# A diffusion-backbone layer on one core: the front of the kernel in a new order, and the first head's modulation chunk moved from VectorE to TensorE

## What is computed

```
m = jax.nn.silu(cvec) @ w_mod + b_mod              # 2048 -> 6 x 2048, for c and for c_ctx
sh_a, sc_a, g_a, sh_f, sc_f, g_f = jnp.split(m[..., None, :], 6, axis=-1)
h = _rmsnorm(s, p['norm_pre_mix']) * (1.0 + sc_a) + sh_a
proj = h @ p['w_in']
qkv = jax.nn.silu(_dwconv(proj[..., COL_K:COL_BETA], p['conv_qkv']))
beta, g = _gdn_gates(proj[..., COL_BETA:COL_Z], p['a_log'], p['dt_bias'])
h = jnp.sin(f1 * (z @ w1 + b1))                    # three such layers, then @ w4, times a window
filt = h * jnp.tile(window, (1, 2))
out = jnp.concatenate([o, y], axis=-1) @ p['w_out']
s = s + g_a * _rmsnorm(out, p['norm_post_mix'])    # then the feed-forward sub-layer
```

## Time and profile before

| | us |
|---|---|
| median of 3 runs | 1856.74 (1856.66 to 1858.7) |
| profiled execution, its own time | 1847.59 |
| its span | 1845.9 |
| PE busy | 1695.5 |
| DVE busy | 1190.6 |
| ACT busy | 727.8 |

### The profile page before, as it was taken

The page is one execution under the profiler, slowest core; times in us unless marked ns, Lnnn a source line. Parts: engine busy times, 40 slices in busy tenths (PEclk is TensorE's granted clock), DMA queues, the critical chain, the costliest instruction groups (busy, mean ns, idle before and its releaser), DMA issues.

```text
span 1845.9 us, 30924 instructions
## 1 busy us (share of the span) xinstructions
PE 1695.5 (92%) x11344; PEld 1512.1 (82%) x11344; DVE 1190.6 (65%) x1778; ACT 727.8 (39%) x1199; POOL 124.2 (7%) x231
## 2 busy tenths in 40 slices
PE   4879699998999899999998599999999998999995
PEld 1237598998989798999998388888888888999994
DVE  2545687786878687777787755555555555565464
ACT  2153334434344434443333344444444443333332
POOL 2000201100111101000000000000000001010010
PEclk9979899998999999999999699999999999999998
DMA  9884342523333242532597044445554446676671
GB/s 356 303 328 157 139 155 80 183 99 138 122 131 137 105 154 84 197 115 92 220 346 298 1 181 183 182 182 189 199 197 187 182 182 207 230 267 208 228 238 57
DMA packets 61424, 334.04 MB, mean 181 GB/s; under 512 B 8395, under 2 KB 12550, under 8 KB 33489
## 3 DMA queue, kind: packets, MB, share of 16 engines
q1 hardware_dynamic: 41808, 257.97, 38.2%
q0 software_dynamic: 18656, 70.35, 10.7%
q10 hardware_dynamic: 864, 4.47, 0.7%
HBM read 328.56 MB, written 4.19 MB: 180 GB/s over the span
## 4 chain that ended last, share of the span: by engine, by line
PE 85%; DVE 6%; DMA 4%; ACT 2%; DVEq 1%; issue 1%; ACTq 0%; SPq 0%
PE o L455 13%; PE o L456 13%; PE o L457 13%; PE o L462 9%; PE g L462 9%; PE o L463 4%; PE g L463 4%; PE g L531 2%; PE g L526 2%; PE g L534 2%; DMA xc<-in_xc_t 2%; PE g L795 1%; ACT w_hi L431 1%; DMA w_raw<-in_w_gates_t 1%; DMA w_raw<-in_w_down_t 1%
## 5 line engine op out<-in xcount | busy, mean ns | idle before, releaser
L436 DVE TENSOR_TENSOR w_lo<-w_raw,w_hi 128x2048 fp32r<-128x2048 f32 (+1 forms) x225 | 472.7, 2101 | 244.6 <-ACT w_hi L431 238.0
L431 ACT CAST w_hi<-w_raw 128x2048 fp32r<-128x2048 f32 (+1 forms) x225 | 394.7, 1754 | 362.3 <-PE o L457 331.5
L455 PE MATMUL o<-h_hi,w_hi 128*128 128x256 f32 (+1 forms) x896 | 305.6, 341 | 0.0
L457 PE MATMUL o<-h_hi,w_lo 128*128 128x256 f32 (+1 forms) x896 | 288.1, 322 | 0.0
L456 PE MATMUL o<-h_lo,w_hi 128*128 128x256 f32 (+1 forms) x896 | 287.8, 321 | 0.0
L462 PE MATMUL o<-h_hi_lo,w_hi 128*128 128x512 f32 x704 | 247.2, 396 | 12.6 <-DVE h_hi_lo L1782 12.6
L462 PE MATMUL g<-h_hi_lo,w_hi 128*128 128x512 f32 x704 | 245.1, 394 | 0.0
L455 PE MATMUL o<-ff_hi,w_hi 128*128 128x256 f32 x704 | 202.9, 288 | 11.0 <-ACT w_hi L431 5.7
L457 PE MATMUL o<-ff_hi,w_lo 128*128 128x256 f32 x704 | 202.0, 287 | 0.0
L463 PE MATMUL o<-h_hi_lo,w_lo 128*128 128x256 f32 x704 | 195.9, 278 | 0.0
L463 PE MATMUL g<-h_hi_lo,w_lo 128*128 128x256 f32 x704 | 195.0, 277 | 0.0
(11 more groups left out here) (327 smaller groups left out, 2665.8 us busy)
## 6 DMA issues: line engine op xcount, KB each, us to landing
w_raw<-in_w_ff_t SPq DMA_DIRECT2D x88, 1024.0 KB, 4.9
w_raw<-in_w_heads_t SPq DMA_DIRECT2D x56, 1024.0 KB, 4.8
w_raw<-in_w_down_t SPq DMA_DIRECT2D x64, 704.0 KB, 5.4
w_mod_raw<-in_w_mod_t SPq DMA_DIRECT2D x32, 1024.0 KB, 6.9
w_mod_piece_h<-in_w_mod_t POOLq DMA_DIRECT2D x128, 256.0 KB, 3.1
w_raw<-in_w_out_t SPq DMA_DIRECT2D x16, 1024.0 KB, 4.8
w_mod_tile_o<-in_w_mod_t POOLq DMA_DIRECT2D x16, 1024.0 KB, 5.3
w_mod_piece_d<-in_w_mod_t POOLq DMA_DIRECT2D x64, 256.0 KB, 5.0
```

The source lines that it names most:

```text
L431: e.copy(whi[p.split[j]][:, :size(p)], raw[p.raw[j]][:, :size(p)]).then_inc(hi_ready, 1)
L436: e.tensor_tensor(wlo[p.split[j]][:, :size(p)], raw[p.raw[j]][:, :size(p)], whi[p.split[j]][:, :size(p)].bitcast(F32), ALU.subtract).then_ ...
L455: e.matmul(o, a, xh, start=first, stop=False)
L457: return e.matmul(o, b, xh, start=False, stop=last)
```

## The change

Seven edits, most in the part ahead of head 0:

1. TensorE's front: the filter layers 0 and 1 stand ahead of tile 0; all eight filter products stand in chunk 0; squares stand in chunk 0 and 1; the spectra are cut in halves (one matmul each) and one half stands after each tile of chunks 2 to 5.
2. Squares: ScalarE squares four k-tiles in one instruction into one buffer of four, TensorE sums them with four matmuls in different 32-row groups (the same number, each a quarter as wide in rows), then ScalarE copies the bank and one more matmul adds the groups (`squares_sum`).
3. VectorE does filter products and sums ahead of the constants, the first `mod_columns` and the norm.
4. `kri_f` is two tiles in other places, stored by two DMAs that now stand behind H0's three loads. The engines no longer wait for the store on SyncE ahead of H0; a wait for it stands ahead of the head loop.
5. Two `mraw` buffers now lie in `w_raw` buffers 0 and 1, so SyncE waits for tile 29's use (`mod_used` 30) ahead of H0's loads.
6. Chunk 12: GpSimd loads it as four 1 MiB tiles into one buffer, and TensorE multiplies them inside H0 (`first_chunk`), with the copy, the columns and the bias behind v and q. `first_dve` has no pieces, and `mod0` is gone.
7. `gates_pe`, `gates_act2` and `gates_dve2` stand at other places between H0's pieces. The pieces of chunks 13 to 19 keep their places in the heads.

```diff
-            chunk(0, lambda: mlp(1), lambda: mlp(2), lambda: squares(0, 4), lambda: squares(4, 8))
-            chunk(1, lambda: squares(8, 12), lambda: squares(12, 16), lambda: taps_(0, 2), lambda: taps_(2, 4))
-            chunk(2, lambda: taps_(4, 6), lambda: taps_(6, 8))
-            chunk(3, *(lambda q=q: spectrum(q) for q in range(4)))
-            chunk(4, *(lambda q=q: spectrum(q) for q in range(4, 8)))
-            for m in range(5, 8):
+            def squares(j):
+                pe.wait_ge(xsq_done, j + 1)
+                for kk in range(4):
+                    last = pe.matmul(G[0][32 * kk:32 * kk + 32, :], ONES[:, 0:32], xsq[:, kk], start=(j == 0), stop=(j == 3))
+                last.then_inc(xsq_used, 1)
...
+            def first_chunk(j):
+                pe.wait_ge(first_landed, 16 * (j + 1))
+                for kk in range(4):
+                    last = pe.matmul(G[5][32 * kk:32 * kk + 32, :], cpad[:, 4 * j + kk], mraw_h[:, kk * 512:(kk + 1) * 512],
+                                     start=(j == 0), stop=(j == 3))
+                last.then_inc(first_used, 1)
...
+            mlp(1)
+            chunk(0, lambda: mlp(2), lambda: taps_(0, 3), lambda: taps_(3, 8), lambda: squares(0))
+            chunk(1, lambda: squares(1), lambda: squares(2), lambda: squares(3), squares_sum)
+            for m in range(2, 6):
+                chunk(m, *(lambda n=n: spectrum(n) for n in range(4 * m - 8, 4 * m - 4)))
+            for m in range(6, 8):
                 chunk(m)
...
-            for k in range(0, KT_N, 4):
-                head_piece(pe, H0, 0, 0, "k", k, k + 4)
-                gates_pe(pe, k // 4)
-            head_piece(pe, H0, 0, 1, "v", 0, KT_N)
+            head_piece(pe, H0, 0, 0, "k", 0, 8)
+            first_chunk(0)
+            head_piece(pe, H0, 0, 0, "k", 8, KT_N)
+            first_chunk(1)
+            gates_pe(pe, 1)
+            head_piece(pe, H0, 0, 1, "v", 0, 8)
+            gates_pe(pe, 3)
+            first_chunk(2)
+            head_piece(pe, H0, 0, 1, "v", 8, KT_N)
+            first_chunk(3)
...
             def first_dve():
-                def pc(k0, k1):
-                    head_pieces(v, 0, 0, k0, k1)
...
                 for t in range(3):
                     refill(v, split_lo, H0, 0, t)
                     conv_qkv(H0, 0, t, t, taps[:, 0])
-                    pc(4 + 4 * t, 8 + 4 * t)
+                    if t == 0:
+                        gates_dve2(1)
                     conv_silu(0, t)
+                    gates_dve2((3, 5, None)[t])
...
+            for j in range(4):
+                if j:
+                    g.wait_ge(first_used, j)
+                g.dma_start(mraw_h[:], A["w_mod_t"][48 + j]).then_inc(first_landed, 16)
+            g.wait_ge(first_used, 4)
...
             stream(GA)
+            sp.wait_ge(mod_used, 30)
+            stream(H0)
             sp.wait_ge(fl_act, 11)
-            sp.dma_start(kri_d, kri_f[:].rearrange("p a c n -> p (a c) n")).then_inc(kri_out, 16)
-            sp.wait_ge(kri_out, 16)
-            for p in (H0, Hf, H, HT, W0):
+            for part in range(2):
+                sp.dma_start(kri_d[:, 8 * part:8 * part + 8], kri_f[part][:].rearrange("p f c n -> p (f c) n")).then_inc(kri_out, 16)
+            for p in (Hf, H, HT, W0):
```

More of the change, by code:

```diff
@@ L610, in filter_taps_pe, with filter_dft_pe @@
                       start=True, stop=True).then_inc(fl_pe, 1)
-        def filter_dft_pe(pe, q):
+        def filter_dft_pe(pe, q, t):
             part, f, n = q // 4, (q // 2) % 2, q % 2
-            if q == 0:
-                pe.wait_ge(fl_dve, 12)
-            if q >= 3:
-                pe.wait_ge(fl_act, q + 1)
-            for t in range(2):
-                last = pe.matmul(G[3 + q % 3][:, :], dft_f[:, part, t, f * P:(f + 1) * P], ab[:, part, t, n * 512:(n + 1) * 512],
-                                 start=(t == 0), stop=(t == 1))
-            last.then_inc(fl_pe, 1)
+            if t == 0:
+                if q == 0:
+                    pe.wait_ge(fl_dve, 12)
+                if q >= 3:
+                    pe.wait_ge(fl_act, q + 1)
+            last = pe.matmul(G[3 + q % 3][:, :], dft_f[:, part, t, f * P:(f + 1) * P], ab[:, part, t, n * 512:(n + 1) * 512],
+                             start=(t == 0), stop=(t == 1))
+            if t:
+                last.then_inc(fl_pe, 1)
         def hyena_forward(pe, q):
@@ L787, in gates_part, with squares_sum @@
                 return last
-            pe.wait_ge(cs_ready, 1)
-            def squares(k0, k1):
-                for k in range(k0, k1):
-                    pe.wait_ge(xsq_done, k + 1)
-                    pe.matmul(G[0][:, :TOK], ONES, xsq[:, k % 2], start=(k == 0), stop=(k == KT_N - 1)).then_inc(xsq_used, 1)
+            def squares(j):
[3 more added lines that the diff above has]
+                last.then_inc(xsq_used, 1)
+            def squares_sum():
+                pe.wait_ge(xsum_rows, 1)
+                pe.matmul(G[2][:, :], ONES, rr[:, 2], start=True, stop=True).then_inc(xsum_done, 1)
             def mlp(l):
@@ L822, in _ @@
             last.then_inc(w_used, 1)
-            for k in range(0, KT_N, 4):
-                head_piece(pe, H0, 0, 0, "k", k, k + 4)
-                gates_pe(pe, k // 4)
-            head_piece(pe, H0, 0, 1, "v", 0, KT_N)
+            head_piece(pe, H0, 0, 0, "k", 0, 8)
[8 more added lines that the diff above has]
+            first_chunk(3)
             head_piece(pe, H0, 0, 2, "q", 0, KT_N)
+            pe.wait_ge(rows_out, 9)
+            for b in range(4):
+                last = pe.matmul(G[4][:, b * 2:(b + 1) * 2], rows[:, b * P:(b + 1) * P], sel[:], start=True, stop=True)
+            last.then_inc(rows_t, 1)
             head_pe(pe, Hf, 0, 0, 0, 0)
@@ L1096, in first_act @@
                     evac_qkv(H0, 0, t, 0, t, taps[:, 0, 5 * t + 2:5 * t + 3])
+                    if t == 1:
+                        act.wait_ge(rows_t, 8)
+                        act.wait_ge(first_used, 4)
+                        act.copy(rows[:], G[5][:, :]).then_inc(rows_out, 1)
                     conv_tanh(0, t)
+                    if t == 0:
+                        gates_act2()
             def head_act(p, i, j0, g, u):
@@ L1510, in _ @@
                 filter_mlp_dve(v, l)
+            for s in range(8):
+                filter_taps_dve(v, s)
+            filter_sums_dve(v)
             v.wait_ge(consts_in, 16 * N_CONST)
```

106 lines of the change are left out of this document (51 added, 55 removed).

## The result

The changed kernel takes 1833.16 us (median of 4 runs, 1824.85 to 1836.39) against 1856.70 us for the kernel before (median of 4, 1849.51 to 1858.7, run beside it). The ratio is 0.988 with a 95% interval of 0.9849 to 0.9912. The forecast was 1826, the range 1818 to 1839: the direction and the range held, and the forecast is 7 us too low. As a gain, 30.3 us were forecast and 23.5 measured, and the interval of the ratio is 16 to 28 us, so the 30.3 lie outside it. The profiled execution took 1834.43 us.

A forecast was written before the change was run, and what follows sets the result against it. The front was held bound by TensorE's order mid-stream, DMA at the stream's ends, then ScalarE's and VectorE's chain to head 0. Savings of 18 + 0 + 10.8 + 1.5 = 30.3 us off 1856.7 gave 1826 us, range 1818 to 1839.

The forecast's parts named there:

- term 1: Stream of modulation tiles at the front: TensorE stays ahead of the DMA, the stream stays full at 416 GB/s, saving 18 us.
- term 4: Start of head 0: chunk 12's column step and VectorE's wait for it and pieces go, saving 1.5 us.
- rival (a): Whole front: both gains, the stream's and head 0's inputs', come, giving 1819 to 1833 us; chance 0.72.
- Rival (b): Middle of the tile stream: TensorE falls to half clock and the stream doesn't fill, giving 1833 to 1845 us; chance 0.13.
- Rival (c): Tile stream: held at 358 GB/s, leaving 10.2 us of its gain and a time of 1834 us; chance 0.04.
- Term 2: Ahead of H0: moving the spectra store neither wins nor costs, 0 us, as the gates product sets when k's product starts.
- T: Moment when TensorE starts k's product for head 0, forecast to stay 13.9 us behind the gates product's start.
- Term 3: Head 0's inputs: from k's product to head 0's start ("tok") takes 45.6 us against 56.4, saving 10.8 us.
- the sign: Head 0's inputs: TensorE's waits for late tiles sum to 1 to 3 us; 5 us or more in one refutes it.
- the walk: Step-by-step sum of durations from k's product through v and q to head 0's start, giving 45.6 us.
- Rival (d): Head 0's inputs: late-tile reloads cost more than the pieces; 1856 to 1862 us, chance 0.03; milder 1833 to 1846, 0.06.
- The distance from profile to median: Whole kernel: the median of runs lies 9.1 us above the profiled execution, carried over unchanged to the forecast.

The follow-up runs named there:

- e1: Kernel before with only chunk 12's multiplication moved inside H0 and the gate steps at their new places; median 1846.4 us, ratio 0.9948 to the kernel before.
- e2: Changed kernel without the chunk 12 and gate-step edits, so the new front alone; median 1836.16 us, ratio 0.9903 to the kernel before.
- e3: Changed kernel plus five unused 128-row matmuls on TensorE ahead of the first filter product; profiled span 1827.2 us.
- e4: Changed kernel with two buffers for the squares instead of one; profiled span 1827.5 us.
- e5: Changed kernel with the two spectra stores and the wait for them put back ahead of H0's loads; profiled span 1824.3 us.
- e11: e3 with the gates tile loaded ahead of tile 24 and ten of sixteen gates-product steps put between tiles 26 to 31; profiled span 1826.4 us.
- e12: Edits of e3, e4, e11, two late-tile buffers, late tiles 2 and 3 behind q, stores between H0 loads, earlier H0 split; 1817.01 us, 0.9807 to the kernel before.
- e9: e3 with the five added matmuls cut to 64 rows of operands; profiled span 1832.7 us.

## Why the prediction was right, and where it was off

**The direction and the two large gains** were right, and e1 and e2 show each by itself. The sum was 30.3 us; the stages show 23.8 at the feed-forward. 4.5 us of the difference are term 1's and 1.5 are term 4's; the last half a us is within what stages differ by from one execution to the next. The result, 1833.16 us, is inside the range of 1818 to 1839, but at the very edge of the 1819 to 1833 that rival (a), both gains come, was to give.

**Term 1, 18 us: the mechanism right, the size off by 4.5 us.** Measured: 13.5. The step that failed reads "That is 8 x 0.96 us warm, and about twice that at the half clock, so tile 3 is used at about 43 us". I took a mixture; all eight products ran at half rate, and tile 3 came at 47.2. The next step, "so 6 us are left before a late use of tile 8 would leave the DMA engines without work", fell with it, since tile 8 was used at 62.0 and not 54. Between tiles 3 and 8 the squares also took turns, which I had priced as four times 0.99 us without ScalarE's 1.91 us ahead of each. e3 shows that the first alone is enough, for with it cured the stream is full and 18.2 us are won; e4 shows that curing the second alone leaves gaps. The stretch missed what a full stream would have moved by (416 - 395) GB/s x 36 us + (416 - 400) GB/s x 60 us = 1.7 MB, which is 4.1 us at 416 GB/s. That is an estimate, and it fits the 4.5.

**Rival (b), the stream doesn't fill for the clock,** was the right suspicion at the wrong place. It was to hit the sixteen tiles with spectra. Those ran at full rate (one tile 1.06, half a spectrum 1.12 us); the filter products ahead of them didn't.

**Rival (c), 358 GB/s,** is excluded: e3's stretch from 52 to 100 us moves 422 GB/s. The Trainium skill ("HBM Reference", Specifications (TRN2)) gives about 425 GB/s for a core that streams alone and the 358 as the share of one of two; the trace agrees with the first.

**Term 2, 0 us,** was right: 13.87 us from the gates product to T after, 13.85 before, and 13.89 in e5 with the store put back. That the three agree so closely is luck. In seven other profiles with the same order of work it is 12.35 to 13.69 us, since TensorE works through the first matmuls of the gates product at half rate for 6.1 us in the changed kernel, and for 2.7 in e1. But "from the gates tile to T nothing else is changed" hid a reserve: e11 and e12 have T earlier than e3 by 3.8 and 4.8 us.

**Term 3, 10.8 us,** was right: "tok" came at T + 45.70, forecast T + 45.6, against T + 56.4. TensorE's weight loads wait 0.7 us in all for late tiles, under the 1 to 3 that were to be the sign. A tenth of a us is closer than the walk was, though. It sent the chain over q's product on TensorE. The chain in the trace goes from v's product (T + 27.5) over ScalarE's and VectorE's split of the next tile and VectorE's convolution of v, and only then, at T + 35.5, to the split ahead of q's convolution. The "about 1 us" that the walk added for v stands where that chain is. Rows of the chain:

```profile
161.22 1.91 ACT w_hi L433
167.07 0.75 DVE v_silu L1320
169.22 1.90 ACT w_hi L433
171.22 2.29 DVE w_lo L438
```
 Rival (d) doesn't show in the changed kernel, and does in e11, for half of that run's loss.

**Term 4, 1.5 us,** isn't there at the end. From head 0's "tok" to head 1's it is 79.74 us before (203.60 to 283.34) and 78.58 after (179.39 to 257.97), 1.2 us less. But later heads with the same instructions differ by up to 2.1 us between these two profiles, and from "tok" to the output projection it takes 699.6 us before and 699.8 after, and 697.4 to 702.4 over all fourteen profiles. Whether it is given back or drowned in that scatter can't be told.

**The distance from profile to median, 9.1 us,** drops out of the forecast, which is the median less the sum. The profiled execution of before had the shorter of the two lengths of the feed-forward (495.7 us), and the three timed ones are 9 to 11 us above it, as if they had the longer. Executions without a profile don't show their stages, so this cause is likely and not shown. The changed kernel's profiled execution had the longer one and lies 1.3 us above its median.

## What to carry to other kernels

Before you price a group of matmuls, see what TensorE did ahead of it in the same trace, and take the duration from a row with the same history, not only the same shape. Where a stream has a fixed number of buffers, ask when the first ones are read: here a late read of tile 3 left the DMA engines at 225 GB/s. A few unused full-size matmuls in idle time can be a very cheap edit: five of them were worth about 5 us. Compare executions by the start of stages that both share. A span mixes your change with the pace of stages that you didn't touch.

## What the runs showed of the hardware

**Two paces of one stage.** The feed-forward, with the same instructions in all kernels, runs at one of two paces for the whole of an execution. In 50 us of it TensorE gets through 290 or 285 matmuls, always busy and with a granted clock of 1.00. These are rows of the kernel before, of the changed kernel, and of e5:

```profile
1149.60:1199.60 50.00, 50.00 (x290) 43.73 (x290) 27.73 (x27) 22.31 (x26) 0.00 (x0) 1.00 0.48 188
```

```profile
1125.80:1175.80 50.00, 50.00 (x285) 43.37 (x284) 27.46 (x26) 21.94 (x28) 0.00 (x0) 1.00 0.53 202
```

```profile
1126.80:1176.80 50.00, 50.00 (x290) 43.71 (x289) 27.72 (x27) 22.33 (x26) 0.00 (x0) 1.00 0.49 191
```

e5 has the changed kernel's front and before's pace, and e1 has before's front and the slow pace (505.1 us), so it isn't the front. The cause stays open.

**64-row matmuls and TensorE's rate.** Behind 16 us of them in the changed kernel and nearly 25 us in e9, each with one tile in between, a product still took about 1.8 us. Behind five 128-row matmuls (6.6 us) it took 0.95, and it stayed at 0.91 to the end of 7.4 us of 64-row work (e3). In the changed kernel and in e9 the durations fell 3 to 6 us after the last product, behind tiles and squares, which have 128 rows. Whether fewer added matmuls would do wasn't tried, and the granted clock reads 1.00 in all these stretches.
